# Cutting the 896 gate or up columns of an expert as 512 + 384 instead of 448 + 448

## The chip, the cores and the metric

The kernel runs on one core of one Trainium2 chip. The metric is the device time of one execution in microseconds, taken as the median of several runs. A profiled execution is a further run, recorded by the hardware profiler.

## What is computed

The kernel computes two transformer-like blocks on 256 tokens of width 1024, in float32. The change touches only the last large part of the second block, a mixture of experts with 8 experts of width 1792, of which each token takes two:

```python
probs = jax.nn.softmax((hf @ w_router).astype(jnp.float32), axis=-1)
vals, idx = lax.top_k(probs, TOP_K)
...
for e in range(N_EXPERTS):
    gate, up = jnp.split(hf @ w_gu[e], 2, axis=-1)      # 1024 -> 2 x 1792
    y = y + combine[:, e:e + 1] * ((jax.nn.silu(gate) * up) @ w_down[e])
```

## The kernel before

The experts run one after another in passes, one expert and at most 128 gathered tokens to a pass; the profiled execution makes 8 passes, the last in code of its own. The weights of an expert come from HBM in 24 chunks. Chunks 0 to 15 hold gate and up columns: the 1792 columns are halved (`j` = 0, 1), each half has a gate and an up part (`part` = 0, 1), and each of these is 896 columns (`EH`) for 1024 rows, in four chunks of two row tiles (`k` = 0, 1). Chunks 16 to 23 hold the rows of the down projection.

Float32 is reached with pairs of reduced-precision numbers. ScalarE copies a chunk to its high part (line 1364, `whi` or `ahi`), VectorE subtracts to get the low part (line 1882, `wlo` or `alo`), and TensorE adds three products: high x high, high x low, low x high. Chunks rotate over six raw slots (`raw`, `ada`) and three pairs of split buffers, so ScalarE may split chunk c + 3 only when TensorE is through with chunk c (semaphore `moe_mm`, raised by the chunk's last matmul), TensorE may begin a chunk when VectorE has raised `moe_lo` for it, and SyncE loads into a raw slot once it has been split.

In a gate or up chunk the tokens are the stationary operand (`hchi`, `hclo`, 128 x 128) and the weights stream. For each of the 2 row tiles and 3 products, two matmuls write to two PSUM banks (line 1288), banks 0 and 1 for gate and 2 and 3 for up: 12 matmuls in 6 pairs a chunk. The stationary operand is loaded again for each matmul. The down projection does the same with 512 columns in each of two banks (line 1315).

When the gate half is complete (chunks 3 and 11), ScalarE reads both banks and writes silu to `sg` (line 1828); when the up half is complete (chunks 7 and 15), VectorE multiplies `sg` with banks 2 and 3 into `ge` (line 2562). TensorE transposes `ge` (line 1263), ScalarE and VectorE split it into `gchi` and `gclo` (line 2492 for the latter), and the down projection starts. TensorE waits for `sg_ready` before it overwrites the gate banks, and for `ge_ready` before it overwrites the up banks. Other instructions that the text names: line 2546, VectorE's scaling of the last pass's result over two banks; line 1368, a ScalarE read of two banks in another stage; lines 774 and 787 to 791, matmuls of earlier stages with 256 and 512 columns.

Of the kernel before, what the change touches and what calls it, by code (L numbers as in the profile page):

```python
# [31 lines left out]
ALU = mybir.AluOpType  # L32
ACT = mybir.ActivationFunctionType
# [30 lines left out]
NE = 8  # L64
ED = 1792
ET = ED // P
EC = ED // 4
EH = ED // 2
MAX_PASSES = NE + 3
SENDS = -(-MAX_PASSES // NT)  # L70
# [232 lines left out]
def blocks(nc, a, out):  # L303

    ctx = ExitStack()
    with ctx:
# [19 lines left out]
        def sem(name):  # L326
            if name not in sems:
                sems[name] = ctx.enter_context(nc.semaphore(name))
            return sems[name]
# [34 lines left out]
        def u(name, cols, dt=F32, parts=P):  # L364
            o = here[0]
            here[0] += (cols * 4 + 31) // 32 * 32
            assert here[0] <= nc.sbuf_usable_end, (name, here[0], nc.sbuf_usable_end)
            return at(name, cols, dt, offset=o, parts=parts)
# [81 lines left out]
        xhi = u("xhi", NT * D, F32R).rearrange("p (t n) -> p t n", t=NT)  # L450
        hc = u("hc", KT * P).rearrange("p (k s) -> p k s", k=KT)
        ge = u("ge", ED)
        sg = u("sg", 2 * EC).rearrange("p (r n) -> p r n", r=2)
        hrow = u("hrow", D)
        drow_at = here[0]
        dchi, dclo = u("dchi", D, F32R), u("dclo", D, F32R)
# [19 lines left out]
        ps = ctx.enter_context(nc.psum_tensor("ps", [P, 8, 512], F32))  # L476
# [278 lines left out]
        def _(pe):  # L755
# [258 lines left out]
            for n, (col, count) in enumerate(VEC_TILES):  # L1014
                m = pe.transpose(ps[:, 5, n * P:n * P + count], rows[0:count, n, :], ident[0:count, 0:count])
# [252 lines left out]
            def expert_pass(p, last):  # L1268

                for j in range(2):  # L1270

                    for part in range(2):
                        if (j, part) == (0, 0):
                            pe.wait_ge(sem("gc_ready"), 4 + 4 * p)
                        elif part == 0:
                            pe.wait_ge(sem("sg_ready"), 1 + 2 * p)
                        elif j == 1:
                            pe.wait_ge(sem("ge_ready"), 3 + 2 * p)
                        for q in range(4):
                            ck = begin_expert(8 * j + 4 * part + q, p)  # L1280
                            if (j, part) == (0, 0) and q % 2 == 0:
                                pe.wait_ge(sem("hc_ready"), 1 + q // 2 + 2 * p)
                            h, l = (view(w[ck.half], 2, EH) for w in (whi, wlo))
                            for k in range(2):
                                kk = 2 * q + k
                                for lhs, rhs in ((hchi, h), (hchi, l), (hclo, h)):
                                    for n in range(2):
                                        m = pe.matmul(ps[:, 2 * part + n, 0:EC], lhs[:, kk], rhs[:, k, n * EC:(n + 1) * EC],  # L1288
                                                      start=(kk == 0 and lhs is hchi and rhs is h),
                                                      stop=(kk == KT - 1 and lhs is hclo))  # L1290
                            m.then_inc(moe_mm, 1)
                            if (j, part, q) == (1, 1, 1):
                                pe.wait_ge(sem("sg_ready"), 2 + 2 * p)
                                turn_gated(0)
                                turn_gated(1)
                        if (j, part) == (0, 1):
                            pe.wait_ge(sem("dc_hi"), 1 + p)
                        if (j, part) == (1, 0) and last:
                            pe.wait_ge(sem("pick_ready"), 2)
                            for t in range(NT):  # L1300
                                m = pe.transpose(ps[:, 4, t * P:(t + 1) * P], pick[:, t, :].bitcast(F32), ident)
                            m.then_inc(sem("pick_turned"), 1)
                if last:
                    pe.wait_ge(sem("pickT_ready"), 1)
                k0 = 0
                for c in range(16, PASS_CHUNKS):
                    kc = expert_shape(c)[0]
                    group = [q for q in range(4) if k0 + kc - 1 in TURNED[q]][0]
                    pe.wait_ge(sem("gc_ready"), (4 + group + 1) + 4 * p)
                    ck = begin_expert(c, p)  # L1310
                    h, l = (view(w[ck.half], kc, D) for w in (whi, wlo))
                    for k in range(kc):
                        for lhs, rhs, stop in ((gchi, h, False), (gchi, l, False), (gclo, h, k0 + k == ET - 1)):
                            for n in range(2):
                                m = pe.matmul(ps[:, 4 + n, :], lhs[:, k0 + k], rhs[:, k, n * 512:(n + 1) * 512],  # L1315
                                              start=(k0 + k == 0 and rhs is h and lhs is gchi), stop=stop)
                    m.then_inc(moe_mm, 1)
                    k0 += kc
                    if c == 16 and not last:
                        turn_gathered(2 + p)  # L1320
                    if c == 17:
                        pe.wait_ge(sem("ge_ready"), 4 + 2 * p)
                        turn_gated(2)
                        turn_gated(3)
# [16 lines left out]
        def _(act):  # L1341
# [343 lines left out]
            for c in range(12):  # L1685
# [12 lines left out]
                b = 6 + c % 2  # L1698
# [124 lines left out]
            def expert_pass(p, last):  # L1823
                for c in range(PASS_CHUNKS):
                    if c in (3, 11):
                        act.wait_ge(moe_mm, (c + 1) + PASS_CHUNKS * p)
                        act.wait_ge(sem("ge_ready"), (c // 8 + 2) + 2 * p)
                        act.activation(sg, ps[:, 0:2, 0:EC], ACT.Silu).then_inc(sem("sg_ready"), 1)
                    if c == 12 and last:
                        act.wait_ge(sem("pick_turned"), 1)  # L1830
                        act.activation(pickT, ps[:, 4, 0:S], ACT.Copy).then_inc(sem("pickT_ready"), 1)
                    if c == 14:
                        turned_hi(0, p)
                        turned_hi(1, p)
                    if c == 17 and not last:
                        gathered(2 + p)
                    if c == 18:
                        turned_hi(2, p)
                        turned_hi(3, p)
                    if c == 19 and not last:  # L1840
                        gathered_hi(2 + p)
                    if c + 3 < PASS_CHUNKS or not last:
                        split_expert(c + 3, p, PASS_CHUNKS)
                    if c == 3:
                        down_rows(p)
                    if c == 8 and not last:
                        act.wait_ge(sem("gathered_turned"), 1 + p)
                        act.wait_ge(sem("rows_sent"), 16 * 2 * NT)
                        fetch_rows(p)
# [17 lines left out]
        def _(ve):  # L1867
# [686 lines left out]
            def expert_pass(p, last):  # L2554
                for c in range(PASS_CHUNKS):
                    if c in (7, 15):
                        j = c // 8
                        ve.wait_ge(sem("sg_ready"), (j + 1) + 2 * p)
                        ve.wait_ge(moe_mm, (c + 1) + PASS_CHUNKS * p)
                        if j == 0:  # L2560
                            ve.wait_ge(sem("ge_turned"), 4 + 4 * p)
                        ve.tensor_tensor(ge[:, j * EH:(j + 1) * EH].rearrange("p (n c) -> p n c", n=2), sg, ps[:, 2:4, 0:EC], ALU.mult)\
                            .then_inc(sem("ge_ready"), 1)
                    if c == 9 and last:
                        make_pick(p)
                    if c == 14:
                        turned_lo(0, p)
                        turned_lo(1, p)
                    if c == 17 and not last:
                        gathered(2 + p)  # L2570
                    if c == 18:
                        turned_lo(2, p)
                        turned_lo(3, p)
                    if c == 20 and not last:
                        gathered_lo(0, 3 + 2 * p)
                        gathered_lo(1, 4 + 2 * p)
                    if c + 3 < PASS_CHUNKS or not last:
                        split_expert(c + 3, p, PASS_CHUNKS)
                    if c == 1:
                        down_gated(p)  # L2580
                    if c in (2, 4) and last:
                        rows_of_choices(c // 4)
                    if c in (12, 15, 18, 21) and last:
                        take_row(c // 18, c // 3 % 2)
# [118 lines left out]
```

## Time and profile before

| | |
|---|---|
| median of 3 runs | 1308.85 us (1307.53 to 1310.15) |
| profiled execution, its own time | 1311.39 us |
| its span, first to last instruction | 1309.3 us |
| granted TensorE clock, mean | 0.982 |
| TensorE busy | 1253.6 us, 96% |
| VectorE busy | 1027.9 us, 79% |
| ScalarE busy | 792.0 us, 60% |
| read from and written to HBM | 360.72 and 14.70 MB |

The engines run side by side, so their busy times don't add up to the span. A matmul is pipelined with its neighbours, and its recorded duration overlaps theirs: the distance between two starts tells the rate. PE is TensorE's matmul, PEld its weight load, DVE is VectorE, ACT is ScalarE, SP is SyncE. A clock of 1.00 is full speed.

### The profile page before, as it was taken

What the parts mean: (1) busy time and instruction counts of PE and PEld (TensorE: products, weight loads), DVE (VectorE), ACT (ScalarE), POOL (GpSimd) and SP (SyncE); (2) the same over time, 40 slices, a digit from 0 to 9 for tenths busy, and PEclk for the clock granted to TensorE, in tenths of its full rate; (3) what the DMA queues carried; (4) which work ended last, traced back from release to release, by engine and by line L of the source; (5) the groups of instructions that cost most, each with busy time, mean ns of one, the idle gap of its engine ahead of it and who ended that gap; (6) DMA issues with size and microseconds to landing.
All of it is one profiled execution on the core that took longest, in us unless ns stands there. A gap on an engine that the chain in (4) does not pass through costs nothing.

```text
span 1309.3 us, 20254 instructions
## 1 busy us (share of the span) xinstructions
PE 1253.6 (96%) x7618; PEld 1112.9 (85%) x7618; DVE 1027.9 (79%) x1100; ACT 792.0 (60%) x1018; POOL 88.7 (7%) x111
## 2 busy tenths in 40 slices
PE   6989999999899999999999998999999999999996
PEld 5978999987889799998888667888888898989884
DVE  6887799896754577786836559898988889898987
ACT  5774566544544554443436665777777777777774
POOL 0020000000462100000001302000000000000020
PEclk9998999999989999999999998999999999999999
DMA  9952897679863569988974135999999999999992
GB/s 316 332 216 97 271 329 267 230 292 256 188 178 102 188 212 331 313 300 323 341 259 155 47 113 207 411 382 386 375 362 388 364 395 353 397 351 410 346 410 82
DMA packets 163835, 369.04 MB, mean 282 GB/s; under 512 B 24404, under 2 KB 96415, under 8 KB 157367
## 3 DMA queue, kind: packets, MB, share of 16 engines
q1 hardware_dynamic: 157201, 350.73, 75.4%
q10 hardware_dynamic: 5094, 12.11, 2.6%
q0 software_dynamic: 1472, 5.28, 1.1%
q8 instruction: 46, 0.75, 0.2%
q14 instruction: 22, 0.18, 0.0%
HBM read 360.72 MB, written 14.70 MB: 287 GB/s over the span
## 4 chain that ended last, share of the span: by engine, by line
PE 72%; DVE 13%; ACT 5%; issue 4%; DMA 2%; POOL 1%; SPq 1%; ACTq 0%; DVEq 0%
PE ps L1288 21%; PE ps L774 7%; PE ps L775 7%; PE ps L776 7%; PE ps L1315 6%; PE ps L787 4%; PE ps L791 4%; PE ps L789 4%; PE ps L848 3%; DVE wlo L1882 3%; DVE wlo L1875 1%; DVE alo L1882 1%; PE ps L922 1%; ACT probs L1486 1%; DMA raw<-in_moe_w_gu 1%
## 5 line engine op out<-in xcount | busy, mean ns | idle before, releaser
L1875 DVE TENSOR_TENSOR wlo<-raw,whi 128x1024 fp32r<-128x1024 f32 x194 | 237.9, 1251 | 95.8 <-ACT whi L1351 92.8
L1351 ACT ACTIVATE whi<-raw 128x1024 fp32r<-128x1024 f32 x194 | 201.6, 1058 | 178.4 <-PE ps L776 117.7
L774 PE MATMUL ps<-ahi,whi 128*128 128x256 f32 x864 | 248.8, 288 | 2.6 <-DVE alo L1907 2.4
L775 PE MATMUL ps<-alo,whi 128*128 128x256 f32 x864 | 246.6, 285 | 0.0
L776 PE MATMUL ps<-ahi,wlo 128*128 128x256 f32 x864 | 246.5, 285 | 0.0
L1882 DVE TENSOR_TENSOR wlo<-raw,whi 128x1792 fp32r<-128x1792 f32 (+1 forms) x96 | 199.3, 2089 | 26.3 <-ACT whi L1364 25.3
L1364 ACT ACTIVATE whi<-raw 128x1792 fp32r<-128x1792 f32 (+1 forms) x96 | 166.9, 1755 | 58.5 <-PE ps L1288 30.5
L774 PEld LDWEIGHTS ps<-ahi,whi 128*128 128x128 f32 x864 | 168.2, 195 | 4.2 <-issue 3.8
L775 PEld LDWEIGHTS ps<-alo,whi 128*128 128x128 f32 x864 | 168.1, 195 | 0.7 <-issue 0.7
L776 PEld LDWEIGHTS ps<-ahi,wlo 128*128 128x128 f32 x864 | 168.0, 194 | 0.0
L1288 PE MATMUL ps<-whi,hchi 128*128 128x448 f32 x352 | 103.6, 376 | 4.8 <-DVE hclo L2439 3.3
L1288 PE MATMUL ps<-wlo,hchi 128*128 128x448 f32 x352 | 100.8, 368 | 0.0
L1288 PE MATMUL ps<-whi,hclo 128*128 128x448 f32 x352 | 100.8, 368 | 0.0
L1288 PEld LDWEIGHTS ps<-whi,hchi 128*128 128x128 f32 x352 | 64.7, 190 | 16.8 <-DVE wlo L1882 6.7
L1882 DVE TENSOR_TENSOR alo<-raw,ahi 128x1792 fp32r<-128x1792 f32 (+1 forms) x32 | 66.8, 2088 | 10.6 <-ACT ahi L1364 10.5
L1288 PEld LDWEIGHTS ps<-whi,hclo 128*128 128x128 f32 x352 | 66.7, 190 | 5.4
L1288 PEld LDWEIGHTS ps<-wlo,hchi 128*128 128x128 f32 x352 | 66.7, 190 | 5.3
L1364 ACT ACTIVATE ahi<-ada 128x1792 fp32r<-128x1792 f32 (+2 forms) x32 | 51.1, 1598 | 29.1 <-PE ps L1288 18.7
L1882 DVE TENSOR_TENSOR alo<-ada,ahi 128x1792 fp32r<-128x1792 f32 (+2 forms) x32 | 60.4, 1888 | 7.9 <-ACT ahi L1364 7.9
L848 PE MATMUL ps<-hx,raw 128*128 128x128 f32 (+1 forms) x512 | 64.9, 290 | 0.6 <-ACT hx L1442 0.4
L848 PEld LDWEIGHTS ps<-hx,raw 128*128 128x128 f32 (+1 forms) x512 | 63.1, 199 | 2.2 <-issue 1.6
L1882 DVE TENSOR_TENSOR wlo<-ada,whi 128x1792 fp32r<-128x1792 f32 (+2 forms) x32 | 60.5, 1889 | 4.7 <-ACT whi L1364 4.3
(346 smaller groups left out, 2409.5 us busy)
## 6 DMA issues: line engine op xcount, KB each, us to landing
raw<-in_moe_w_gu SPq DMA_DIRECT2D x96, 896.0 KB, 7.0
ada<-in_w_ada SPq DMA_DIRECT2D x48, 1024.0 KB, 7.2
raw<-in_moe_w_down SPq DMA_DIRECT2D x32, 1024.0 KB, 7.6
ada<-in_moe_w_gu SPq DMA_DIRECT2D x32, 896.0 KB, 7.3
raw<-in_w_up SPq DMA_DIRECT2D x22, 1024.0 KB, 6.2
raw<-in_ffn_w_gu SPq DMA_DIRECT2D x22, 1024.0 KB, 8.6
ada<-in_moe_w_down SPq DMA_DIRECT2D x16, 1024.0 KB, 8.8
raw<-in_na_w_qkv SPq DMA_DIRECT2D x12, 1024.0 KB, 8.1
```

The source lines that it names most:

```text
L774: pe.matmul(o, h[:, k, cols], bhi[:, k], start=(k == 0), stop=False)
L775: pe.matmul(o, h[:, k, cols], blo[:, k], start=False, stop=False)
L776: m = pe.matmul(o, l[:, k, cols], bhi[:, k], start=False, stop=(k == KT - 1))
L787: pe.matmul(o, bhi[at_k][:, tok], h[:, k, n0:n0 + n], start=first, stop=False)
L789: pe.matmul(o, bhi[at_k][:, tok], l[:, k, n0:n0 + n], start=False, stop=False)
L848: m = pe.matmul(o[:, t * P:(t + 1) * P], w[:, k, cols], hx[:, t, k], start=(k == 0), stop=(k == KT - 1))
L1288: m = pe.matmul(ps[:, 2 * part + n, 0:EC], lhs[:, kk], rhs[:, k, n * EC:(n + 1) * EC], start=(kk == 0 and lhs is hchi and rhs is h), stop= ...
L1315: m = pe.matmul(ps[:, 4 + n, :], lhs[:, k0 + k], rhs[:, k, n * 512:(n + 1) * 512], start=(k0 + k == 0 and rhs is h and lhs is gchi), stop= ...
L1351: act.activation(high_, src, ACT.Copy).then_inc(hi_done, 1)
L1364: act.activation(whi[ck.half][:, 0:k * n], raws[ck.slot][:, 0:k * n], ACT.Copy).then_inc(moe_hi, 1)
L1875: ve.tensor_tensor(low_, src, high_.bitcast(F32), ALU.subtract).then_inc(lo_done, 1)
L1882: ve.tensor_tensor(wlo[ck.half][:, 0:k * n], raws[ck.slot][:, 0:k * n], whi[ck.half][:, 0:k * n].bitcast(F32), ALU.subtract).then_inc(moe_ ...
```

## The change

A pair of matmuls over 896 columns was cut in the middle, 448 columns at the start of each bank. Now the first matmul of a pair writes the whole of its bank, 512 columns, and the second writes 384 to the start of the next bank. The 896 results then lie one behind the other across the two banks, and the reads of ScalarE and VectorE, formerly two runs of 448, are one run of 896. `sg` has the same size as before.

```diff
--- before.py
+++ after.py
@@ -64,7 +64,7 @@
 NE = 8
 ED = 1792
 ET = ED // P
-EC = ED // 4
+EC = [(0, 512), (512, ED // 2 - 512)]
 EH = ED // 2
 MAX_PASSES = NE + 3
 SENDS = -(-MAX_PASSES // NT)
@@ -450,7 +450,7 @@
         xhi = u("xhi", NT * D, F32R).rearrange("p (t n) -> p t n", t=NT)
         hc = u("hc", KT * P).rearrange("p (k s) -> p k s", k=KT)
         ge = u("ge", ED)
-        sg = u("sg", 2 * EC).rearrange("p (r n) -> p r n", r=2)
+        sg = u("sg", EH)
         hrow = u("hrow", D)
         drow_at = here[0]
         dchi, dclo = u("dchi", D, F32R), u("dclo", D, F32R)
@@ -1284,8 +1284,8 @@
                             for k in range(2):
                                 kk = 2 * q + k
                                 for lhs, rhs in ((hchi, h), (hchi, l), (hclo, h)):
-                                    for n in range(2):
-                                        m = pe.matmul(ps[:, 2 * part + n, 0:EC], lhs[:, kk], rhs[:, k, n * EC:(n + 1) * EC],
+                                    for n, (n0, count) in enumerate(EC):
+                                        m = pe.matmul(ps[:, 2 * part + n, 0:count], lhs[:, kk], rhs[:, k, n0:n0 + count],
                                                       start=(kk == 0 and lhs is hchi and rhs is h),
                                                       stop=(kk == KT - 1 and lhs is hclo))
                             m.then_inc(moe_mm, 1)
@@ -1825,7 +1825,7 @@
                     if c in (3, 11):
                         act.wait_ge(moe_mm, (c + 1) + PASS_CHUNKS * p)
                         act.wait_ge(sem("ge_ready"), (c // 8 + 2) + 2 * p)
-                        act.activation(sg, ps[:, 0:2, 0:EC], ACT.Silu).then_inc(sem("sg_ready"), 1)
+                        act.activation(sg, ps[:, 0:2, :].rearrange("p b n -> p (b n)")[:, 0:EH], ACT.Silu).then_inc(sem("sg_ready"), 1)
                     if c == 12 and last:
                         act.wait_ge(sem("pick_turned"), 1)
                         act.activation(pickT, ps[:, 4, 0:S], ACT.Copy).then_inc(sem("pickT_ready"), 1)
@@ -2559,7 +2559,7 @@
                         ve.wait_ge(moe_mm, (c + 1) + PASS_CHUNKS * p)
                         if j == 0:
                             ve.wait_ge(sem("ge_turned"), 4 + 4 * p)
-                        ve.tensor_tensor(ge[:, j * EH:(j + 1) * EH].rearrange("p (n c) -> p n c", n=2), sg, ps[:, 2:4, 0:EC], ALU.mult)\
+                        ve.tensor_tensor(ge[:, j * EH:(j + 1) * EH], sg, ps[:, 2:4, :].rearrange("p b n -> p (b n)")[:, 0:EH], ALU.mult)\
                             .then_inc(sem("ge_ready"), 1)
                     if c == 9 and last:
                         make_pick(p)
```

## Rows read from the trace of the kernel before

**Rows 1.** The page: span, busy time by engine, the chain's shares by line.

```profile
span 1309.3 us, 20254 instructions
...
PE 1253.6 (96%) x7618; PEld 1112.9 (85%) x7618; DVE 1027.9 (79%) x1100; ACT 792.0 (60%) x1018; POOL 88.7 (7%) x111
...
PE ps L1288 21%; PE ps L774 7%; PE ps L775 7%; PE ps L776 7%; PE ps L1315 6%; PE ps L787 4%; PE ps L791 4%; PE ps L789 4%; PE ps L848 3%; DVE wlo L1882 3%; DVE wlo L1875 1%; DVE alo L1882 1%; PE ps L922 1%; ACT probs L1486 1%; DMA raw<-in_moe_w_gu 1%
```

**Rows 2.** Table by stretch, one full pass; counts in brackets, then clock, DMA share, GB/s.

```profile
974.82:1036.23 61.41, 61.22 (x298) 53.80 (x299) 55.11 (x38) 46.02 (x38) 0.00 (x0) 1.00 1.01 379
```

**Rows 3.** The chain, one pass: start us, us, engine, tile, line, count.

```profile
861.80 34.52 PE ps L1288 x168
...
897.08 4.87 PE ps L1288 x24
...
913.39 9.82 PE ps L1315 x42
```

**Rows 4.** Weight loads: by line with min/median/max ns; by group with busy and mean ns.

```profile
L1288 PEld LDWEIGHTS ps<-whi,hchi x352: 186/188/333, 796.4 to 1270.1; 128*128 128x128 f32 x176
...
L774 PEld LDWEIGHTS ps<-ahi,whi 128*128 128x128 f32 x864 | 168.2, 195 | 4.2 <-issue 3.8 <-ACT qT L1592 0.4
```

**Rows 5.** Timeline of TensorE, line 1288, first and last of 28 pairs.

```profile
883.99 0.56 PE L1288 MATMUL ps<-whi,hchi 128*128 128x448 f32 x2
...
894.94 0.57 PE L1288 MATMUL ps<-whi,hchi 128*128 128x448 f32 x2
```

**Rows 6.** Timeline of TensorE, 512 columns, first pair and the start 44 pairs on.

```profile
619.97 0.62 PE L789 MATMUL ps<-wlo,ghi 128*128 128x512 f32 x2
...
639.92 0.39 PE L787 MATMUL ps<-whi,ghi 128*128 128x512 f32 x1
```

**Rows 7.** Timeline of TensorE, 256 columns, first and last of 136 single rows.

```profile
499.77 0.28 PE L775 MATMUL ps<-alo,whi 128*128 128x256 f32 x1
...
515.97 0.28 PE L775 MATMUL ps<-alo,whi 128*128 128x256 f32 x1
```

**Rows 8.** Timeline of TensorE, 512 columns in a pass, after a wait.

```profile
913.95 0.63 PE L1315 MATMUL ps<-alo,gchi 128*128 128x512 f32 x2
...
916.26 0.62 PE L1315 MATMUL ps<-whi,gchi 128*128 128x512 f32 x2
...
918.98 0.62 PE L1315 MATMUL ps<-whi,gchi 128*128 128x512 f32 x2
```

**Rows 9.** Waits of one pass: us in total, times, longest.

```profile
ACT whi L1364 <- PE ps L1288: 5.8, 8, 0.9
...
PEld ps L1288 <- DVE wlo L1882: 0.6, 2, 0.3
```

**Rows 10.** Timeline of TensorE, then of ScalarE, around chunks 4 to 6.

```profile
874.12 0.57 PE L1288 MATMUL ps<-ahi,hchi 128*128 128x448 f32 x2
...
876.59 0.67 PE L1288 MATMUL ps<-whi,hchi 128*128 128x448 f32 x2
...
871.97 0.92 ACT L1828 ACTIVATE sg<-ps 128x896 f32<-128x896 f32 x1 [0.81 <-PE ps L1288]
```

**Rows 11.** Timeline of ScalarE, then of VectorE, around the end of chunk 15.

```profile
899.54 1.92 ACT L1364 ACTIVATE ahi<-ada 128x2048 fp32r<-128x2048 f32 x1 [1.26 <-PE ps L1288]
...
901.49 2.29 DVE L1882 TENSOR_TENSOR alo<-ada,ahi 128x2048 fp32r<-128x2048 f32 x1 [1.22 <-ACT ahi L1364]
903.70 1.08 DVE L2562 TENSOR_TENSOR ge<-sg,ps 128x896 f32<-128x896 f32 x1
```

**Rows 12.** Groups by line and shape: busy us, mean ns.

```profile
L1828 ACT ACTIVATE sg<-ps 128x896 f32<-128x896 f32 x16 | 14.7, 921 | 13.2 <-PE ps L1288 13.2
...
L1368 ACT ACTIVATE xn<-ps 128x1024 f32<-128x1024 f32 x4 | 4.1, 1016 | 4.8 <-PE ps L791 4.8
...
L2562 DVE TENSOR_TENSOR ge<-sg,ps 128x896 f32<-128x896 f32 x16 | 17.3, 1081 | 0.0
...
L2546 DVE TENSOR_TENSOR drow<-ps,gvec 128x1024 f32<-128x1024 f32 x8 | 9.7, 1218 | 0.0
```

## The prediction

> **What bounds the kernel now.** I read the page first. TensorE is busy for 96% of the span, and of the chain that ended last the gate and up matmuls of line 1288 are the largest single line, 21% [rows 1]. These are the matmuls that the change reshapes, so I went to their stage. Eight passes over the experts follow one another; the table by stretch shows that one full pass takes 61.4 us, at the full TensorE clock (1.00 granted, its level of 2.4 GHz), with TensorE busy for all but 0.2 us of it and the DMA engines busy throughout [rows 2]. DMA being full is not yet a bound: in the waits of a pass nobody in the matmul path waits for a load, while ScalarE waits for TensorE to give back a buffer [rows 9].
>
> The chain through one pass says where a faster or slower matmul would count [rows 3]: 168 matmuls of line 1288 in one piece (34.52 us), 24 more (4.87 us), then some 11 us that run through VectorE, then 42 matmuls of line 1315 (9.82 us). A matmul's busy time in the profile overlaps its neighbour's, so the durations (0.57 us for two) say nothing of the rate. What counts is the distance between starts, and that is read from the timeline:
>
> - 448 columns: from the row at 883.99 to the row at 894.94 there are 27 pairs, so 10.95 us / 54 = 202.8 ns each [rows 5].
> - 512 columns: from 619.97 to 639.92 there are 44 pairs, 19.95 / 88 = 226.7 ns [rows 6].
> - 256 columns: 135 distances in 515.97 - 499.77 = 16.20 us, 120.0 ns [rows 7].
>
> **The change part by part.** The number of matmuls, of weight loads and of columns stays: 8 passes x 16 chunks x 6 pairs = 768 pairs of 896 columns. Only the cut within a pair moves, so everything hangs on whether the distance between starts is a straight line in the columns. From 256 to 512 columns it rises by (226.7 - 120.0) / 256 = 0.417 ns a column, which leaves 13.3 ns that do not depend on columns. On a straight line the pair costs the same however it is cut. But the 448 rows lie off that line: it gives 120.0 + 192 x 0.417 = 200.0 ns, and 202.8 is measured, 2.8 ns more, through long stretches without a wait. The surplus is not the stage: 512-column matmuls in the same passes settle at 226.7 ns too (918.98 - 916.26 = 2.72 us for 12). They do so only after a start at 231.0 ns (916.26 - 913.95 = 2.31 us for 10) behind a wait [rows 8]. So a matmul has a tighter and a looser rhythm here, and 448 columns never reach the tighter one. No row has 384 columns, or lengths that alternate; the new pair is bounded from both sides:
>
> - before: 2 x 202.8 = 405.6 ns.
> - lowest: both on the line, 226.7 + (226.7 - 128 x 0.417) = 226.7 + 173.3 = 400.0, that is 5.6 less.
> - highest: both in the looser rhythm of the 512 rows, 231.0 + (231.0 - 53.4) = 408.6, that is 3.0 more.
> - taken: both with the surplus of the 448 rows, 202.8 + 26.7 = 229.5 and 202.8 - 26.7 = 176.1, together 405.6: no change. I take this because those are the same lines in the same order of instructions, and the row nearest to 384 columns.
>
> The Trainium skill (TensorE: Matmul & The Clock Gate, Back-to-back issue gap) gives the isolated distance as columns / 2.4 GHz plus a fixed 2.5 ns. By that rule the pair is 378 ns before and after and any gain is excluded. The trace agrees on the slope and not on the fixed part, which is 13.3 ns on two lengths and 16.0 on the third; that unevenness is what the rival below lives on.
>
> Next, how much of a pair's difference reaches the end. A chunk is 6 pairs, so the low end makes it 34 ns shorter. Not every chunk counts. After chunk 3 ScalarE first makes silu (871.97, 0.92 us), then splits chunk 6, VectorE subtracts, and TensorE starts chunk 6 at 876.59 [rows 10]. Six pairs of 0.4055 from chunk 5's start at 874.12 would be 876.55, so the split is already late there, and its weight load, which could not start ahead, stretches the first pair of chunk 6 (0.67 us busy against 0.57). Chunks 4 and 5 run in the shadow of ScalarE and VectorE, and what they gain is waited away. The same holds for chunk 0, in front of the other of the two waits per pass for the split weights (0.6 us in both) [rows 9]. Chunk 15 doesn't count either: VectorE's multiply that follows it at 903.70 waits behind a subtraction (901.49, 2.29 us) that hangs on ScalarE's split (899.54), and so on the end of chunk 14 [rows 11]. That leaves 12 chunks of 16, 576 pairs in all. The last pass is looser than the others, so this is rather too many. The low end is then 576 x -5.6 ns = -3.2 us (-4.3 if all 768 counted), the high end 768 x 3.0 = +2.3 us at most and 576 x 3.0 = +1.7 on the same count.
>
> The two reads of PSUM become one run of 896 instead of two of 448. Both have a row of 1024 elements over two banks in one run beside them. ScalarE's silu takes 921 ns, the 1024-wide read 1016; in proportion 896 would take 889, which is below what it can be since a fixed part is in it, and 921 is above. Halfway, 905, is 16 ns less, and one silu of the two per pass is on the path: 8 x 16 = -0.1 us (0 to -0.3). VectorE's multiply takes 1081, the 1024-wide one 1218, in proportion 1066: at most 15 ns less, behind which other VectorE work is queued; taken as nothing [rows 12]. The last matmul of a chunk starts later by what its shorter stream saves, so chunks complete as before and no wait moves. Slots, loads and the split sizes are untouched. The DMA engines stay full; a pass shorter by 0.4 us in 61.4 asks 0.7% more of them, and ScalarE's freedom from load waits says there is that much.
>
> Sum: 0 (pairs) - 0.1 (silu) = -0.1 us. The profiled execution took 1311.39 us around a span of 1309.3; the median of the runs is 1308.85, 2.5 us below it, and differences are put on the median: 1308.7.
>
> **The rivals.**
>
> *The tight rhythm.* 512 and 384 are both multiples of 128, 448 is not, and every length that reaches the tight rhythm here (256, 512) is such a multiple. If that is the reason, the pair falls to 400.0 and the time to 1308.85 - 3.2 - 0.1 = 1305.5. Against it: two lengths make no rule, and here they alternate, so each matmul follows one of another length. Chance 0.24. If only the 512 half gets it (226.7 + 176.1 = 402.8, -2.8 a pair), -1.6 us: 1307.1. Chance 0.11.
>
> *The loose rhythm.* The alternation keeps the pair at 408.6: +1.7 us, 1310.5. Chance 0.09.
>
> *The weight load comes out from behind the short matmul.* This is the one that ends slower. Every matmul here has its own load of 128 x 128; it starts with the matmul before and is recorded at 188 ns [rows 4]. 384 columns stream for 384 x 0.417 = 160 ns. If the recorded load time is a floor, then the 448 rows' 202.8 ns are at that floor, the 384-column half stays at 202.8 and the pair is 226.7 + 202.8 = 429.5, +23.9 ns. Per pass 96 x 23.9 = 2.3 us, less about 0.35 us that the two waits of [rows 9] give back, times 8: +15.6 us, 1324.4. Against it: the same recorded loads of 195 ns stand before 256-column matmuls that start every 120.0 ns [rows 4, 7], so most of the recorded time overlaps. It decides (over 0.2%, 2.6 us) once the 384-column half passes 405.6 - 226.7 + 2600 / 576 = 183.4 ns. The Trainium skill (same page, LDWEIGHTS) puts a load at columns / 1.2 GHz, 107 ns for 128, which 160 ns of streaming would cover. Chance 0.04.
>
> **How the numbers follow.** No change in the pair: 0.52, 1308.7, own range 1307.5 to 1310.1. Runs of one kernel lie within 2.6 us of each other, so 0.2% (2.6 us) is about what can be told from no change. The range runs from the tight rhythm to a little beyond the loose one, 1305.3 to 1311.0, and leaves out the exposed load, the case in which all 768 pairs gain, and scatter. Faster by over 0.2% needs under 1306.2: about two thirds of the tight rhythm's 0.24, and a little of the half case: 0.20. Slower needs over 1311.5: the exposed load and a part of the loose rhythm with scatter: 0.10. The rest is 0.70.
>
> **What the profile after would show.** From the start of a pair of line 1288 to the start two pairs on: 0.811 us if I am right, 0.800 in the tight rhythm, 0.817 in the loose one, 0.859 with the load exposed. A pass of 61.4 us stays within 0.1; the tight rhythm makes it 61.0. The wait before chunk 6 grows by some 0.07 us if chunks get shorter. Silu takes 889 to 921 ns, the multiply no less than 1066. I am wrong if the distance of a 384-column matmul to the next start lies outside 173 to 178 ns, if alternating lengths cost something that neither length alone shows, or if a pass changes by more than the pairs do.

## The result and the profile after

| | before | after |
|---|---|---|
| median of 10 runs each | 1308.60 us (1304.90 to 1312.56) | 1313.08 us (1308.15 to 1316.69) |
| ratio, 95% interval | | 1.0037 [1.0022, 1.0051] |
| profiled execution, own time | 1311.39 us | 1308.15 us |
| its span | 1309.3 us | 1306.2 us |

The change makes the kernel slower, by 0.37%; the medians lie 4.5 us apart. The two profiled executions say the opposite if only their spans are read, so the reading has to go by stages.

The page of the kernel after [rows 1]:

```profile
span 1306.2 us, 20254 instructions
...
PE 1253.1 (96%) x7618; PEld 1100.1 (84%) x7618; DVE 1028.2 (79%) x1100; ACT 792.2 (61%) x1018; POOL 88.7 (7%) x111
```

TensorE's busy time hardly moves, 1253.6 us before and 1253.1 after. A matmul's busy time overlaps its neighbour's, so it cannot show this. The table by stretch for one pass [rows 2]:

```profile
970.31:1032.25 61.94, 61.81 (x298) 52.68 (x299) 55.24 (x38) 46.05 (x37) 0.00 (x0) 1.00 1.00 372
```

A pass takes 61.94 us, 0.53 more, still at a clock of 1.00, with TensorE busy for all but 0.13 us and VectorE and ScalarE busy as long as before within 0.13 us. The chain, with the passes that follow each other [rows 3]:

```profile
856.23 35.02 PE ps L1288 x168
...
918.18 35.02 PE ps L1288 x168
...
953.96 4.95 PE ps L1288 x24
...
1227.84 10.21 PE ps L1288 x48
```

The 168 matmuls in one piece take 35.02 us in place of 34.52 and the 24 take 4.95 in place of 4.87. The last pass of before begins here:

```profile
1230.29 10.07 PE ps L1288 x48
```

From the first of these pieces to the last pass, six passes, before took 1230.29 - 861.80 = 368.49 us and after took 1227.84 - 856.23 = 371.61: 3.1 us more. That the profile after is nevertheless the shorter one is decided ahead of the passes, where the code is the same: the first weight load of line 1288 starts at 791.0 us after the change and at 796.4 before [rows 4]. The medians, not these two executions, say how the kernels compare.

The timeline of TensorE in the gate and up matmuls, first pair of a stretch and first half of its last [rows 5]; with narrower windows the two halves of a pair come apart:

```profile
878.69 0.58 PE L1288 MATMUL ps<-whi,hchi 128*128 128x512 f32 x2
...
889.85 0.40 PE L1288 MATMUL ps<-whi,hchi 128*128 128x512 f32 x1
```

```profile
889.44 0.40 PE L1288 MATMUL ps<-whi,hclo 128*128 128x512 f32 x1
...
889.68 0.34 PE L1288 MATMUL ps<-whi,hclo 128*128 128x384 f32 x1
```

From 878.69 to 889.85 there are 27 pairs, 11.16 us, so a pair takes 413.3 ns, against 405.6 between the rows of before [rows 5] and 405.4 as the mean over the chunks of its full passes. The start of a 384 comes 0.24 us after that of its 512, and the next 512 follows 0.17 us later. So the short matmul is not the one that costs: it stays near the 173 to 176 ns that I gave it. The 512-column one takes some 237 ns to the next start, more than in any row that I had read.

The readers of PSUM, and the wait of TensorE for split weights in one pass [rows 12, 9]:

```profile
L2562 DVE TENSOR_TENSOR ge<-sg,ps 128x896 f32<-128x896 f32 x16 | 17.3, 1081 | 0.0
...
L1828 ACT ACTIVATE sg<-ps 128x896 f32<-128x896 f32 x16 | 14.7, 921 | 14.4 <-PE ps L1288 14.4
```

```profile
PEld ps L1288 <- DVE wlo L1882: 0.5, 2, 0.3
```

Silu and the multiply take exactly what they took, 921 and 1081 ns. The joined run of 896 is worth nothing.

### The profile page after: what moved, and what is told of

Same layout as the page of the kernel before. It is cut to its first block, busy times and chain, and to the rows that moved or that the text cites. A ratio compares the mean times of both kernels' runs of the same rounds, so it can differ in the third digit from the quotient of the medians.

```text
span 1306.2 us, 20254 instructions
## 1 busy us (share of the span) xinstructions
PE 1253.1 (96%) x7618; PEld 1100.1 (84%) x7618; DVE 1028.2 (79%) x1100; ACT 792.2 (61%) x1018; POOL 88.7 (7%) x111
## 4 chain that ended last, share of the span: by engine, by line
PE 71%; DVE 14%; ACT 5%; issue 4%; DMA 3%; POOL 1%; SPq 1%; ACTq 0%; DVEq 0%
PE ps L1288 20%; PE ps L774 7%; PE ps L775 7%; PE ps L776 7%; PE ps L1315 6%; PE ps L787 4%; PE ps L791 4%; PE ps L789 4%; PE ps L848 3%; DVE wlo L1882 3%; DMA raw<-in_moe_w_gu 2%; DVE alo L1882 1%; DVE wlo L1875 1%; PE ps L922 1%; ACT probs L1486 1%
## 5 line engine op out<-in xcount | busy, mean ns | idle before, releaser
L1288 PE MATMUL ps<-whi,hchi 128*128 128x512 f32 x352 | 104.3, 377 | 4.2 <-DVE hclo L2439 3.3
L1288 PE MATMUL ps<-whi,hclo 128*128 128x512 f32 x352 | 102.0, 370 | 0.0
L1288 PE MATMUL ps<-wlo,hchi 128*128 128x512 f32 x352 | 101.9, 370 | 0.0
```

What stands on the lines that cost most here:

```text
L1288: m = pe.matmul(ps[:, 2 * part + n, 0:count], lhs[:, kk], rhs[:, k, n0:n0 + count], start=(kk == 0 and lhs is hchi and rhs is h), stop=(kk ...
```

## The experiments

A rhythm is here a distance between starts that a stream of matmuls keeps up. Three theories stood first. A: the distance between starts is a property of TensorE's own stream of matmuls, set by their lengths and order. B: TensorE loses the nanoseconds to the other engines and the DMA. C: it is the place of the results in the banks, or the readers.

### Matmuls alone

```diff
+for i in range(60):
+    m = pe.matmul(ps[:, i % 2, 0:(512, 384)[i % 2]], A[:, i // 2 % 8 * P:(i // 2 % 8 + 1) * P],
+                  W[:, (0, 512)[i % 2]:(512, 896)[i % 2]], start=True, stop=True)
+pause(m, 8)   # GpSimd answers, then the next run of another cut
```

> Only matmuls with their weight loads, in runs of 60 without a wait, each run with its own cut (256/256 to 512/512, 512/384, 384/512, 480/416 and others); no other engine works beside them, and nothing of the two blocks is computed. Theory A (the distance between starts is a property of TensorE's own stream, set by the lengths and their order): 448/448 starts every 202.7 ns here too, 512/512 every 226.7, and a pair of 512/384 takes 413 ns against 405 for 448/448. Theory B (TensorE loses the extra nanoseconds to ScalarE, VectorE or DMA at the same memory): all cuts fall on the straight line, 200.0 for 448, 400.0 for each pair of 896 columns. Theory C (an unequal pair costs nothing by itself, the cost is in the place of the results in the banks or in the readers): 512/384 as 448/448.

The chain shows each run as one row with its start, length and line. In this order: 384/384, 448/448, 512/512, 512/384, 384/512, 480/416.

```profile
36.13 10.69 PE ps L80 x60
...
58.79 12.45 PE ps L88 x60
...
84.82 13.91 PE ps L96 x60
...
98.94 12.67 PE ps L100 x60
...
111.81 12.48 PE ps L104 x60
...
124.50 12.30 PE ps L108 x60
```

A row holds some 0.3 us beyond its 60 distances (512/512: 13.91 - 60 x 0.2267 = 0.31). Less that, the pairs take 346 ns (384/384), 405 (448/448), 412 (512/384), 406 (384/512) and 400 (480/416). Two lengths that each lie on the straight line when alone, 384 at 10.38 / 60 = 173 and 512 at 227, leave it when they alternate, and 480 with 416 gains. Theory B expected 400 for each of these pairs with the other engines at rest, and 448/448 keeps its 405; theory C expected 512/384 to equal 448/448, with the same banks and no readers in each run.

Theory A's 413 for 512/384 isn't firm either. Two more runs of 512/384 in this execution, one of them with the second piece read from column 1024, took 12.49 and 12.47 us, that is some 406 ns a pair, as 384/512 did.

> The same runs of matmuls, with ScalarE copying 128x2048, VectorE subtracting 128x2048 and SyncE loading 1 MB pieces without a stop beside them; nothing of the two blocks is computed. Theory A: each run as without the others, within 1 ns. Theory B: 448/448 at 202.7 and the 512/384 pair at 413 only here. Theory C: as without the others, 512/384 equal to 448/448.

How busy the others were, and the runs 448/448 and 512/384:

```profile
20.00:160.00 140.00, 137.40 (x709) 122.57 (x707) 137.96 (x61) 137.74 (x72) 1.25 (x12) 1.00 1.01 421
```

```profile
57.90 12.44 PE ps L103 x60
...
98.17 12.66 PE ps L115 x60
```

VectorE and ScalarE were busy for 98% of that stretch and the DMA engines for all of it, and the rows are those of the quiet run within 0.02 us, 512/384 at 413 ns with them. Of the other runs in that stretch only 480/480 differs by more, 13.28 us against 13.18. B falls.

### Inside the kernel: readers, dose, order

The cut of before, with results joined (against the kernel before; VectorE's read is moved in the same way):

```diff
-EC = ED // 4
+EC = [(0, 448), (448, ED // 2 - 448)]
+AT = 512 - 448
...
+m = pe.matmul(ps[:, 2 * part + n, AT * (1 - n):AT * (1 - n) + count], lhs[:, kk], rhs[:, k, n0:n0 + count],
...
+act.activation(sg, ps[:, 0:2, :].rearrange("p b n -> p (b n)")[:, AT:AT + EH], ACT.Silu)
```

> The kernel of before with its cut of 448 and 448, but the first piece at the end of its bank, so that the 896 results lie in one run and the readers read one run as after the change. Theory A: pairs of 405.4 ns, passes of 61.4 us, the time of before within 0.2%. Theory C: slower by 0.3 to 0.4% as after the change, passes of 61.9 us.

Measured: 1309.37 us, ratio 1.0003 [0.9990, 1.0017]. Four of its six full passes take 61.40 us, like this one:

```profile
921.55 34.52 PE ps L1289 x168
...
982.95 34.52 PE ps L1289 x168
```

So the joined results and the single read cost nothing that the runs can tell. C falls.

The other two passes take 61.54 and 61.56 us. In them, from the wait for split weights before chunk 1 to the one before chunk 6, 448/448 runs slowly:

```profile
863.02 0.57 PE L1289 MATMUL ps<-wlo,hchi 128*128 128x448 f32 x2
...
874.59 0.57 PE L1289 MATMUL ps<-ahi,hclo 128*128 128x448 f32 x2
```

(874.59 - 863.02) / 28 = 413.2 ns a pair, in a program that has no other cut. The trace of the kernel before has the same rhythm in its first pass, at a granted clock of 1.00, and again in its last:

```profile
802.04 0.57 PE L1288 MATMUL ps<-whi,hclo 128*128 128x448 f32 x2
...
805.76 0.57 PE L1288 MATMUL ps<-ahi,hclo 128*128 128x448 f32 x2
```

(805.76 - 802.04) / 9 = 413.3 ns. The loose rhythm that the change shows is thus no product of unequal lengths: the cut of before has it too, but for short stretches, while the change has it nearly throughout.

Only the up columns cut 512 and 384 (against the kernel after; ScalarE reads two runs again):

```diff
+EC_GATE = [(0, ED // 4), (ED // 4, ED // 4)]
...
-for n, (n0, count) in enumerate(EC):
+for n, (n0, count) in enumerate(EC if part else EC_GATE):
```

> The gate columns cut 448 and 448 as before, the up columns 512 and 384 as after. Theory A: half of the pairs at 413 ns, a pass of 61.65 to 61.7 us, slower than before by about 0.2%. Theory C with the readers at fault: only VectorE's read is changed, so the pass moves by nothing or by the whole.

Measured: 1312.28 us, ratio 1.0020 [1.0007, 1.0034]. The ratio is that of half a dose, but the profile is not: its six full passes take 2.4 us more than those of before, where the change's take 3.1. The passes last between 61.53 and 61.96 us, and in a long one the gate matmuls, cut 448 and 448, run like this (first and last of 16 pairs):

```profile
944.09 0.57 PE L1289 MATMUL ps<-ahi,hclo 128*128 128x448 f32 x2
...
950.29 0.57 PE L1289 MATMUL ps<-whi,hclo 128*128 128x448 f32 x2
```

(950.29 - 944.09) / 15 = 413.3 ns a pair, for the cut of before. In the six full passes the gate columns of the second half follow what the up columns ahead of them do: slow behind 413 ns, 405 behind 407. My expectation of a plain half dose was wrong.

The same lengths in the other order, once by issue order alone, once with 384 columns first in the weights row and in the banks (both against the kernel after; the second also moves the results and the reads by `AT`, as above):

```diff
-for n, (n0, count) in enumerate(EC):
+for n, (n0, count) in reversed(list(enumerate(EC))):      # swapped
```

```diff
-EC = [(0, 512), (512, ED // 2 - 512)]
+EC = [(0, 384), (384, ED // 2 - 384)]                     # 384 first
+AT = 512 - 384
```

> The change as it is, but in each pair the matmul of 384 columns is issued before the one of 512. The same lengths alternate, so Theory A says the same two values are open as in the run alone, 406.7 or 413.3 ns a pair: a pass of 61.5 to 61.95 us. A theory that the extra time comes from the order (a long stream directly in front of the next product's first matmul) says 405 ns or less.

> Cut 384 and 512, the 384 columns at the end of the first bank and issued first. Theory A: as with the swapped order, 406.7 or 413.3 ns a pair, a pass of 61.5 to 61.95 us, between no change and 0.4% slower than before. If the place of the pieces in the banks or in the weights row mattered, it would differ from the swapped order.

Measured: swapped 1310.72 us, ratio 1.0009 [0.9993, 1.0025]; 384 first 1310.82 us, ratio 1.0023 [1.0004, 1.0042]. The chain of the second, from two places, shows both rhythms in one execution: 982.66 - 920.76 = 61.90 us for a pass, then 1106.09 - 1044.59 = 61.50.

```profile
920.76 35.02 PE ps L1289 x168
...
982.66 35.01 PE ps L1289 x168
...
1044.59 34.61 PE ps L1289 x168
...
1106.09 34.61 PE ps L1289 x168
```

The six full passes of the swapped order take 61.50 to 61.82 us. The theory that the order alone costs the time asked for 405 ns or less, that is passes of at most 61.4, and falls. The swapped median can't be told from that of before, though, and whether the order makes the slow rhythm rarer one profile each can't tell. Within these full passes a rhythm changes only where TensorE had waited (before chunk 1 or chunk 6) or done other matmuls (before chunk 14).

### More cuts, and how firm a rhythm is

> Runs of 80 matmuls alone, nothing of the two blocks is computed: 512/384 six times and 384/512 twice, each behind a wait, 480/416 three times, and the cuts 416/480, 496/400, 488/408, 472/424, 504/392, 400/400, 352/352. Theory A with two rhythms: each 512/384 run settles at 406.7 or at 413.3 ns and at nothing else, 480/416 at 400.0 each time, 448/448 at 405.3 each time. If 512/384 gives other values too, there are more than two rhythms.

Runs of 80. In this order: 512/384 (second of six), 480/416 (first of three), 488/408, 448/448 (first of two), 512/384 (sixth).

```profile
35.11 16.81 PE ps L76 x80
...
86.15 16.33 PE ps L88 x80
...
152.62 16.29 PE ps L104 x80
...
202.63 16.81 PE ps L116 x80
...
287.43 16.55 PE ps L136 x80
```

A row again holds some 0.28 us beyond its 40 pairs, so 16.81 is a pair of 413 ns, 16.55 one of 407 and 16.3 one of 400. Of the six runs of 512/384, the one that follows other matmuls without a wait took 16.27 us (it has no such 0.28: 407 ns), four took 16.81 and one 16.55, and 384/512 took 16.81 once and 16.54 once. Both runs of 448/448 took 16.81 here, where the same run took 405 ns a pair before. 480/416 gave 400 each time and 488/408 gave 400; its mirror 416/480 took 16.48 us, 405 ns, and 496/400 16.54, 407 ns. There are at least four rhythms for 896 columns, at 400, 405, 407 and 413 ns, and a cut can have more than one.

> The change itself, once more. Theory E (the rhythm is fixed by what stands around the matmuls in the program, so it comes back in each execution): pairs of 413.3 ns and passes of 61.95 us in this profile too, ratio to before 1.002 to 1.005. Theory F (it is drawn anew by each execution): another mixture of 406.7 and 413.3, passes between 61.5 and 61.95 us.

> The kernel of before, once more, for its profile. Theory E: pairs of 405.3 ns and passes of 61.4 us again. Theory F: some passes with 448/448 at 413.3 ns, the rhythm that this pair showed when alone.

The chain of the change again, then of before again (its one long pass):

```profile
924.01 35.02 PE ps L1288 x168
...
985.97 35.02 PE ps L1288 x168
...
1109.88 34.62 PE ps L1288 x168
...
1171.44 35.03 PE ps L1288 x168
```

```profile
1167.13 34.66 PE ps L1288 x168
...
1228.70 29.85 PE ps L1288 x144
```

The change: 1311.12 us, ratio 1.0020 [1.0004, 1.0036], with passes of 61.96 us as in its first profile, but one of 61.56 (1171.44 - 1109.88) among them. Before: five passes of 61.40 to 61.44, and this one of 61.57, with 448/448 at 413.3 ns in its chunks 1 to 5. Theory E holds for most passes: the rhythm of the last execution comes back. It doesn't hold for each: single passes draw another, as theory F has it, and not the same ones in each execution.

### Is it the weight load?

```diff
-m = pe.matmul(ps[:, i % 2, ...], A[:, i // 2 % 8 * P:(i // 2 % 8 + 1) * P], ...
+m = pe.matmul(ps[0:64, i % 2, ...], A[:, i // 2 % 8 * P:i // 2 % 8 * P + 64], ...
```

> Matmuls alone in runs of 80, nothing of the two blocks is computed: 512/384 three times, 448/448 twice, 480/416, 512/512 and 384/384, each with weights of 128, then 64, then 32 columns. Theory G (the rhythms come from the weight load that runs beside each matmul): with 64 or 32 columns the loads are shorter, and the rhythms of 405.3, 406.7 and 413.3 give way to 400.0 for every cut. Theory H (they come from the streams themselves or from how starts are handed over): the same values with fewer weight columns.

Runs of 80. With 128 weight columns: 512/384 (second of three), 480/416, 512/512; with 64: 512/384 (third); with 32: 512/384 (third), 480/416, 512/512.

```profile
35.02 16.54 PE ps L76 x80
...
101.93 16.29 PE ps L92 x80
...
118.42 18.45 PE ps L96 x80
...
184.72 16.36 PE ps L112 x80
...
317.52 16.45 PE ps L144 x80
...
367.35 16.48 PE ps L156 x80
...
384.03 18.72 PE ps L160 x80
```

The loads are shorter indeed: recorded at 188, 134 and 108 ns. The start of a run takes less time with narrower weights, so a row is shorter by up to 0.1 us for that alone (read from 384/384, whose rhythm is taken as unchanged). Beyond it, 512/384 falls a little with 64 columns, to (16.36 - 0.22) / 40 = 403 or 404 ns (384/384 at this width took 14.09 us, 0.22 more than 80 x 173.3 ns), and is back at 407 with 32. 480/416 leaves its 400 and rises to 407, and 512/512 goes from 18.45 us to 18.72. 448/448 goes from 16.50 us to 16.41 and 16.38, which is 1 ns a pair. Theory G asked for 400 from every cut; it falls. Theory H asked for the same values, and 480/416 and 512/512 don't keep theirs. The edit also narrows what a matmul writes (`ps[0:64]`), so the runs don't say whether load or output shifts them. The 413 ns rhythm came up at no width in this execution, 128 included; whether it survives a shorter load isn't shown.

The first row also bears on what chooses a rhythm. Up to it TensorE has the same instructions in this kernel and in the runs of 80 before: 30 matmuls, a run of 512/384, a wait, a second run of 512/384. Here the second run took 16.54 us, there 16.81. So the same instructions gave 407 ns in one execution and 413 in another, and the program ahead of a run does not settle its rhythm.

### A cut that gains

> Cut 480 and 416, the first piece at the end of its bank so that readers still read one run. Theory A (the distance between starts depends on the lengths and their order alone): alternating 480/416 took 400.0 ns a pair in the run of matmuls alone, so pairs of 400 ns here against 405.4 before and 413.4 after the change; a pass of 61.0 to 61.1 us, 3 to 4 us faster than before (ratio near 0.9975). Theory D (any unequal pair costs extra inside the kernel, with its waits at each chunk): passes above 61.4 us, slower than before.

> Cut 488 and 408, results again in one run. In the run of matmuls alone this pair took 400.0 ns, as 480/416 did. Theory A: pairs of 400.0 ns in the kernel, passes of 61.1 us as with 480/416 (0.32 us below before), 2 to 2.5 us faster than before in all, ratio near 0.998. A theory that 480 is good because it is a multiple of 32 or 96 says more than 400.

The edit is that of the joined 448 cut, with 480 or 488 in its place. 480: 1307.63 us, ratio 0.9989 [0.9977, 1.0000], so not told from before; I had expected 3 to 4 us. 488: 1306.58 us, ratio 0.9977 [0.9959, 0.9995]. The chain, one pass to the next, of 480 and then of 488:

```profile
920.25 34.24 PE ps L1289 x168
...
981.35 34.24 PE ps L1289 x168
```

```profile
922.84 34.20 PE ps L1289 x168
...
983.91 34.20 PE ps L1289 x168
```

Passes of 61.10 and 61.07 us, 0.32 to 0.35 below before. Six of these make about 2 us, 0.15 to 0.16%, which is what the runs can just tell. Of the two, 488/408 has its interval below 1; that it is the better one isn't shown, the passes differ by 0.03 us. Theory D, that every unequal pair costs extra in the kernel, falls.

488/408 isn't free of the slow rhythm. Its first pass has it through eight chunks:

```profile
826.06 0.57 PE L1289 MATMUL ps<-whi,hchi 128*128 128x488 f32 x2
...
834.33 0.57 PE L1289 MATMUL ps<-whi,hclo 128*128 128x488 f32 x2
```

(834.33 - 826.06) / 20 = 413.5 ns a pair. 480/416 shows none of it in its one profile.

## Why the prediction was wrong

The forecast was 1308.7 us in a range of 1305.3 to 1311.0, and 1313.08 was measured.

*The step that failed* is the bound of the new pair: "highest: both in the looser rhythm of the 512 rows, 231.0 + (231.0 - 53.4) = 408.6". The pair takes 413.3, outside the bracket of 400.0 to 408.6. Two things were wrong in it.

The loose rhythm was mis-sized. I took 231.0 from ten matmuls of 512 columns on their way out of a wait, which then settled at 226.7. The slow rhythm that holds is 413.3 ns a pair, and it is not a property of 512 columns: 448/448, 488/408, 384/512 and 512/384 all have it. The trace of before had it in two places (from 802.04 on, for one), and I read one stretch of 27 pairs and took its 405.6 for the only value. What the change moved is how much of the time TensorE spends in the slow rhythm: short stretches before, nearly all of the passes after.

The sum of two lengths was wrong as well. I gave each length a distance of its own, read from runs of equal lengths. Alone, both do lie where I put them (173 and 227 ns). Alternating they don't add up: even the quicker rhythm of 512/384 is 406.7, not 400.0. The text said that no row has lengths that alternate, and then bounded them by rows that don't. Of my signs of being wrong it was this one that came, a cost that neither length alone shows.

"Taken ... 405.6: no change" fell with both. The 0.09 that I gave to the loose rhythm was the only chance on the right mechanism, at 3.0 ns of its 7.9.

*How much of a pair reaches the end.* The count of 576 pairs of 768 nearly held: 72 pairs a pass x 7.9 ns = 0.57 us, and a pass grew by 0.53. With 480/416, 72 x -5.4 = -0.39 was to come and -0.32 came. So somewhat more than my four chunks of a pass is taken up by waits. For eight passes my own sum with 7.9 ns in it would have been 576 x 7.9 = +4.6 us; six passes show +3.1, and the first and the last hang on loads, so they don't add in proportion. 3.1 us is 0.24%, inside both intervals measured for the change, below the middle of one (0.37%) and above that of the other (0.20%). Whether the medians hold more than the passes show, the profiles can't tell.

*The tight rhythm* existed, but not for my reason. It isn't multiples of 128: 512/384 is made of two and runs at 407 or 413, while 480/416 and, in all its full passes, 488/408 get 400.0.

*The exposed weight load* was wrong: 384/384 starts every 173 ns behind loads recorded at 188, and with loads of 108 ns in place of 188 the pairs of 405 and 407 ns stay within 1 ns.

*The readers*: taken as -0.1 us, measured 0. The silu took 921 ns, the end of its range at which nothing is saved.

*The wait before chunk 6* was to move with the pair; after the change the two waits of a pass are 0.5 us in place of 0.6.

*The rule of the Trainium skill* (TensorE: Matmul & The Clock Gate, Back-to-back issue gap), which for the isolated distance has a fixed part per matmul beside columns / 2.4 GHz, cannot give these results with any fixed part: by it all cuts of 896 columns cost the same, and the runs alone have them at 400, 405, 407 and 413 ns.

What stays open: why TensorE has these rhythms, what chooses one after a wait, and why 512/384 draws the slow one so much more often in the kernel than 448/448 does. The runs rule out other engines and DMA as the cause, and the place of the results in the banks; they rule out the length of the weight load for the steps between 400 and 407 only. No run went without a load for each matmul or kept to one bank. The choice itself was seen and not controlled.

## What to carry to other kernels

A stream of matmuls can have more than one rate for the same sequence of lengths, and none of them need be the sum of what each length costs by itself. Before recutting one, read the distance between starts in many stretches of the trace and not in one: the slow rhythm stood in the trace of before. Then run the bare sequence alone in its loop order, several times, each behind a wait. That showed the values of the kernel, though not how often it takes each, and not the slow rhythm of 488/408, which ran only once. And when an edit is worth 0.3%, compare the stage's own length in the profiles; the whole spans of two executions differed by 3 us in the wrong direction.

## What the runs showed of the hardware

- Pairs of 896 streamed columns with a weight load for each matmul took about 400, 405, 407 or 413 ns at a granted clock of 1.00, by the cut and by the stretch. A sequence holds its rhythm through a run of 80 matmuls; in the full passes of kernels with one cut it changed only behind a wait or behind other matmuls.
- The slow rhythm, 413 ns, came with 448/448, 488/408, 512/384 and 384/512. 448/448 took 405 ns in the first set of runs and 413 in the second, and 413.3 in stretches of the kernel before. The same instructions up to and with a second run of 512/384 gave 407 ns in one execution and 413 in another.
- ScalarE, VectorE and DMA at full load beside it moved TensorE's runs of 9 to 14 us by 0.02 us at most, but for 480/480 (13.28 us against 13.18).
- Narrower weights and output (32 of 128 columns) made 512/512 slower, 18.72 us for 80 matmuls against 18.45, with loads recorded at 108 ns in place of 188.
- A read of PSUM in one run over two banks costs what two runs of half the length in two banks cost: 921 and 1081 ns both ways.
